# Attention in a three-part block: the probabilities turned by ordinary products with the identity instead of transposes

## The chip, the cores and the metric

The kernel runs on one core of a Trainium2 chip. The metric is the device time in microseconds of one execution. The engines are named as in the profile: PE is the matrix engine (PEld its loading of weights, which overlaps the products), DVE the vector engine, ACT the scalar engine, POOL the GpSimd engine, and SP starts the transfers that bring the weights into SBUF.

## What is computed

Three blocks follow each other on 256 tokens of width 1024: a block with three kinds of attention (compressed, selected, window), a block with dilated attention, and a third one with convolution, a gated delta rule and two feed-forward parts. All is float32. The change concerns only how two of the attention stages handle their probabilities. Cut to that, each head computes:

```python
# selected and window attention of the first block: 2 branches x 16 heads;
# dilated attention of the second block: 16 heads
s = jnp.einsum('bcghd,bkgd->bcghk', qq, kk) * scale
p = masked_softmax(s, mask)              # exp(s - max) / sum
o = jnp.einsum('bcghk,bkgd->bcghd', p, vv)
```

With 256 tokens, causality leaves three blocks of 128 queries by 128 keys for each head: the first 128 queries see the first 128 keys, the other 128 queries see all 256.

## The kernel before

The program is written out engine by engine. Each engine has its own list of instructions, and semaphores tie the lists together. A stage is over for PE when its last product is issued. PE goes from one stage to the next in this order: the projections of the first block with their turned operands, the compressed attention, the attention stage `nsa_att`, the output projection, then the same for the second block with `dil_att`, then the third block.

Both attention stages are objects of one class, `Attention`. Its `items` are the heads: 32 items in `nsa_att` (two groups of heads, two branches in each, eight heads) and 16 in `dil_att`. PE's list for them is a software pipeline over i:

- scores of item i (L828, L829): two products, with 64 rows of the array filled, since a head has 64 dimensions. The first makes 128 x 128 scores, the second 128 x 256. They go into bank i % 2 and wait until DVE has read item i - 2 (`masked_done`).
- the turned probabilities of item j = i - 2 (L837, 838): three blocks of 128 x 128 into bank 2 + j % 2, after ACT's exponentials of that item (`exp_done`) and after the turned blocks of item j - 2 have been copied out (`probsT_ready`). The probabilities are the weights that are loaded, the identity is the moving operand. The text below calls this group T(j).
- the products with v of item i - 3 (L849, L850, L851): three products with 64 moving columns each, whose weights are the turned probabilities. They add up in banks 4 to 7.

In the last iterations of a stage there are no scores left, so T and the products with v follow each other.

Beside it, DVE adds the mask to the scores and takes the maximum (L864, L866), makes the bias (L869), does one step of the modulation sums per item (`ada_beside`, L567), and copies out the turned blocks of every second item; after each eight items it weighs the sums (L1074, L1306). ACT does the exponentials (L891, L893) and copies out the turned blocks of the other items. These copies carry the line L527 of a helper. The next steps after the last item are a weighting on DVE, in the first stage an addition on POOL, and then the turning of the result and the output projection.

In all places other than this class, the kernel turns blocks in the helper `turn` with L514. The third block's delta rule contains ordinary products of 128 x 128 by 128 (L1940, L1945, L1994, L2002, L2010) and with 16 rows (L1930).

Of the kernel before, what the change touches and what calls it, by code (L numbers as in the profile page):

```python
# [12 lines left out]
P = 128  # L13
# [270 lines left out]
def build(nc, A, const_ap, out, last_block=2):  # L284
    ctx = ExitStack()
    with ctx:
# [9 lines left out]
        def C(name):  # L296
            a, b = CONST_AT[name]
            return const[:, a:b]

        ident, ones = C("ident"), C("ones")  # L300
# [28 lines left out]
        bank = [ctx.enter_context(nc.psum_tensor(f"bank{i}", [P, 512], F32))[:, :] for i in range(8)]  # L329
# [123 lines left out]
        lefts_used = set()  # L453

        def gemm(pe, stage, j, left, ready, n, kc_total=KC):


# [50 lines left out]
        def turn(pe, name, b, blocks):  # L508

            i = TURN_AT[name, b]  # L510
            if i >= 2:
                await_turns_read(pe, TURNS[i - 2][0], [TURNS[i - 2][1]])
            for src, kin, mout, col in blocks:
                mm = pe.transpose(bank[4 + i % 2][0:mout, col:col + kin], src, ident[0:kin, 0:kin])  # L514
            mm.then_inc(turned, 1)
# [280 lines left out]
        class Attention:  # L796
# [24 lines left out]
            def pe(self, pe):  # L821
                n = len(self.items)
                for i in range(n + 3):
                    if i < n:
                        q, k, _, _ = self.items[i]
                        if i >= 2:
                            pe.wait_ge(self.masked_done, i - 1)
                        pe.matmul(bank[i % 2][:, 0:P], q(0), k()[:, 0:P], start=True, stop=True)  # L828
                        pe.matmul(bank[i % 2][:, P:3 * P], q(1), k(), start=True,  # L829
                                  stop=True).then_inc(self.scored, 1)  # L830
                    if 2 <= i < n + 2:
                        j = i - 2
                        pe.wait_ge(self.exp_done, j + 1)
                        if j >= 2:
                            pe.wait_ge(self.probsT_ready[j % 2], j // 2)
                        for b in range(3):
                            mm = pe.transpose(bank[2 + j % 2][:, b * P:(b + 1) * P],  # L837
                                              self.probs[:, j % 2, b * P:(b + 1) * P], ident)
                        mm.then_inc(self.probs_turned, 1)
                    if i >= 3:  # L840
                        j = i - 3
                        g, c = j // 8, (j % 8) * DH
                        pe.wait_ge(self.probsT_ready[j % 2], j // 2 + 1)
                        if j % 8 == 0 and g >= 2:
                            pe.wait_ge(self.pv_read, g - 1)
                        v = self.items[j][3]
                        pT = self.probsT[:, j % 2, :]
                        o0, o1 = bank[4 + 2 * (g % 2)], bank[5 + 2 * (g % 2)]
                        pe.matmul(o0[:, c:c + DH], pT[:, 0:P], v(0), start=True, stop=True)  # L849
                        pe.matmul(o1[:, c:c + DH], pT[:, P:2 * P], v(0), start=True, stop=False)  # L850
                        pe.matmul(o1[:, c:c + DH], pT[:, 2 * P:3 * P], v(1), start=False,  # L851
                                  stop=True).then_inc(self.pv_done, 1)
# [1561 lines left out]
```

## Time and profile before

| | |
|---|---|
| median of 3 runs | 1487.2 us (1487.14 to 1492.58) |
| the profiled execution | 1491.99 us, span 1490.2 us |
| mean granted clock of PE | 0.862 of full speed |
| busy share of the span | PE 86%, PEld 71%, DVE 60%, ACT 35%, POOL 18% |
| instructions | PE 7557 products and 7557 weight loads, DVE 1465, ACT 875, POOL 154 |
| bytes from HBM | 219.27 MB, 148 GB/s over the span |

The profile shows one execution. Times are microseconds from the start of the span. A row of the timeline gives start, length, engine, line, operation, tiles, shape and the number of records it merges (x3); the length of a merged row runs from the first start to the last end. For a product the shape reads rows x columns of the weights, then the moving operand. "granted clock" is the share of PE's full clock that the chip allowed; its two levels are 0.5 (1.2 GHz) and 1.0 (2.4 GHz).

### The profile page before, as it was taken

How to read it: one execution, taken by the hardware profiler on the slowest of the kernel's cores; microseconds unless marked ns; L12 is line 12 of the kernel's file. 1: busy time of each engine (PE TensorE's matmuls, PEld its weight loads, DVE VectorE, ACT ScalarE, POOL GpSimd, SP SyncE). 2: the span in 40 equal slices, each digit the busy share in tenths (PEclk: the TensorE clock that was granted, in tenths of full speed). 3: DMA queues.
4: the chain of work that ended last, by engine and by line, in shares of the span. 5: the costliest groups of instructions: out<-in, count | busy, mean ns of one | idle time of the engine just before them, and what ended most of it. 6: DMA issues, size and time to landing. Idle time of an engine off the chain costs nothing. (4 is left out here: it accounts for less than half of the span.)

```text
span 1490.2 us, 19544 instructions
## 1 busy us (share of the span) xinstructions
PE 1275.6 (86%) x7557; PEld 1051.1 (71%) x7557; DVE 900.9 (60%) x1465; ACT 520.7 (35%) x875; POOL 264.5 (18%) x154
## 2 busy tenths in 40 slices
PE   1789699977888986999997988899989879799997
PEld 1565567765766764788785767678888877688885
DVE  5783556535985556595555578468655555555553
ACT  1231333323224333334433433533323233444441
POOL 0010001003542003334202432211030302100000
PEclk9989755578999557999998998879989989899998
DMA  8667342213776213487563444439600014455551
GB/s 290 237 226 243 102 126 73 71 43 112 229 242 208 98 57 110 154 291 230 182 201 104 135 123 127 142 123 300 240 2 2 3 58 142 127 177 183 197 164 71
DMA packets 142391, 221.59 MB, mean 149 GB/s; under 512 B 9735, under 2 KB 65627, under 8 KB 142171
## 3 DMA queue, kind: packets, MB, share of 16 engines
q1 hardware_dynamic: 139424, 216.37, 45.1%
q10 hardware_dynamic: 2875, 3.98, 0.8%
q8 instruction: 60, 0.98, 0.3%
q14 instruction: 32, 0.26, 0.1%
HBM read 219.27 MB, written 1.05 MB: 148 GB/s over the span
## 5 line engine op out<-in xcount | busy, mean ns | idle before, releaser
L479 PE MATMUL bank<-w_parts,lhs_hi 128*128 128x512 f32 (+2 forms) x960 | 397.5, 414 | 24.3 <-ACT w_parts L433 24.3
L433 ACT CAST w_parts<-ring 128x1024 fp32r<-128x1024 f32 (+2 forms) x288 | 288.9, 1033 | 344.9 <-PE bank L480 138.7
L438 DVE TENSOR_TENSOR w_parts<-ring,w_parts 128x1024 fp32r<-128x1024 f32 (+2 forms) x230 | 309.8, 1373 | 162.5 <-ACT w_parts L433 162.0
L480 PE MATMUL bank<-w_parts,lhs_lo 128*128 128x512 f32 (+2 forms) x960 | 390.6, 407 | 0.0
L487 PE MATMUL bank<-w_parts,lhs_hi 128*128 128x512 f32 (+2 forms) x960 | 262.8, 396 | 3.2 <-DVE w_parts L438 3.2
L479 PEld LDWEIGHTS bank<-w_parts,lhs_hi 128*128 128x128 f32 x960 | 191.2, 199 | 67.3 <-ACT w_parts L433 25.9
L480 PEld LDWEIGHTS bank<-w_parts,lhs_lo 128*128 128x128 f32 x960 | 191.8, 200 | 40.2
L487 PEld LDWEIGHTS bank<-w_parts,lhs_hi 128*128 128x128 f32 x960 | 184.9, 193 | 45.5 <-DVE w_parts L438 4.1
L438 POOL TENSOR_TENSOR w_parts<-ring,w_parts 128x1024 fp32r<-128x1024 f32 (+1 forms) x58 | 147.9, 2551 | 248.9 <-ACT w_parts L433 248.9
L567 DVE SCALAR_TENSOR_TENSOR ada_acc<-ring,c_act,ada_acc 128x512 f32<-128x512 f32 x210 | 172.9, 823 | 12.2 <-DMA ring<-in_w_ada 1.1
L762 POOL TENSOR_TENSOR x<-x,xn 128x512 f32<-128x512 f32 x20 | 30.1, 1524 | 415.3 <-DVE xn L754 415.3
L514 PE MATMUL bank<-const,arena 128*128 128x128 f32 (+2 forms) x322 | 58.0, 330 | 33.0 <-DVE arena L1336 6.8
L514 PEld LDWEIGHTS bank<-const,arena 128*128 128x128 f32 (+2 forms) x322 | 46.6, 172 | 42.8 <-DVE arena L1336 7.0
L590 PE MATMUL bank<-const,ada_acc 128*128 128x1 f32 x160 | 26.0, 284 | 50.5 <-DVE ada_acc L567 39.9
L479 PE MATMUL bank<-w_parts,up_hi 128*128 128x512 f32 x176 | 69.2, 393 | 0.0
L480 PE MATMUL bank<-w_parts,up_lo 128*128 128x512 f32 x176 | 68.7, 391 | 0.0
L1412 DVE TENSOR_TENSOR arena<-arena,bank 128x256 f32<-128x256 f32 x44 | 18.1, 420 | 83.0 <-ACT arena L1428 82.3
L590 PEld LDWEIGHTS bank<-const,ada_acc 128*128 128x128 f32 x160 | 25.8, 240 | 55.0 <-DVE ada_acc L567 35.3
L891 ACT ACTIVATE arena<-arena 128x128 f32<-128x128 f32 x48 | 19.3, 402 | 110.7 <-DVE arena L869 110.6
L514 PE MATMUL bank<-const,xn 128*128 128x128 f32 x80 | 19.8, 429 | 42.5 <-DVE xn L676 36.6
L864 DVE CUSTOM_DVE_ANT_0 arena<-bank,const 128x128 f32<-128x128 f32 x48 | 14.0, 291 | 66.3 <-PE bank L829 66.1
L1428 ACT ACTIVATE arena<-bank 128x256 f32<-128x256 f32 x44 | 16.8, 384 | 91.2 <-PE bank L487 89.6
(321 smaller groups left out, 1692.6 us busy)
## 6 DMA issues: line engine op xcount, KB each, us to landing
ring<-in_w_ffn_up SPq DMA_DIRECT2D x176, 256.0 KB, 3.8
ring<-in_w_ada SPq DMA_DIRECT2D x72, 512.0 KB, 4.7
ring<-in_ada_w SPq DMA_DIRECT2D x48, 512.0 KB, 4.8
ring<-in_w_ffn_down SPq DMA_DIRECT2D x44, 512.0 KB, 4.3
ring<-in_w_in SPq DMA_DIRECT2D x44, 512.0 KB, 4.0
ring<-in_dil_w_in SPq DMA_DIRECT2D x32, 512.0 KB, 4.1
ring<-in_nsa_w_in SPq DMA_DIRECT2D x20, 512.0 KB, 4.6
ring<-in_w_in SPq DMA_DIRECT2D x20, 416.0 KB, 4.2
```

Source lines behind the costliest of these rows:

```text
L433: eng.copy(hi, raw).then_inc(hi_ready, 1)
L438: eng.tensor_tensor(lo, raw, hi.bitcast(F32), ALU.subtract).then_inc(lo_ready[who], 1)
L479: pe.matmul(b, x_hi, w, start=(k0 + k == 0), stop=False)
L480: mm = pe.matmul(b, x_lo, w, start=False, stop=False)
L487: mm = pe.matmul(bank[2 * (o % 2) + tt][:, 0:n], x_hi, lo[:, k * n:(k + 1) * n], start=False, stop=(k0 + k == kc_total - 1))
L514: mm = pe.transpose(bank[4 + i % 2][0:mout, col:col + kin], src, ident[0:kin, 0:kin])
L567: ins = dve.scalar_tensor_tensor(acc, w, s, acc, ALU.mult, ALU.add)
L590: mm = pe.matmul(bank[7][:, c:c + 1], acc[:, c * P:(c + 1) * P], ones[:, 0:1], start=True, stop=True)
L762: pool.tensor_tensor(xs, xs, y_gated[:, tt, :], ALU.add).then_inc(x_ready, 1)
L891: act.activation(p[:, 0:P], m[:, 0:P], ACT.Exp, bias=self.bias[:, i, 0:1], scale=SCALE, accum_out=self.den[:, i, 0:1])
L1412: dve.tensor_tensor(up_h[:, j % 2, tt, :], up_a[:, j % 2, tt, :], gemm_bank(name + "_up", j, tt)[:, 256:512], ALU.mult).then_inc(bank_free ...
L1428: act.activation(up_a[:, j % 2, tt, :], gemm_bank(name + "_up", j, tt)[:, 0:256], ACT.Silu).then_inc(silu_done, 1)
```

## The change

In the turning step of the class `Attention`, `pe.transpose` is replaced by an ordinary `pe.matmul` with the same operands in the same roles: the block of probabilities as weights, the identity as moving operand, result into the same part of the same bank, each product starting and stopping its own sum. Waits, semaphores, order and all other engines stay as they are. The other places that turn blocks (`turn`, L514) keep the transpose.

```diff
@@ -834,8 +834,8 @@
                         if j >= 2:
                             pe.wait_ge(self.probsT_ready[j % 2], j // 2)
                         for b in range(3):
-                            mm = pe.transpose(bank[2 + j % 2][:, b * P:(b + 1) * P],
-                                              self.probs[:, j % 2, b * P:(b + 1) * P], ident)
+                            mm = pe.matmul(bank[2 + j % 2][:, b * P:(b + 1) * P],
+                                           self.probs[:, j % 2, b * P:(b + 1) * P], ident, start=True, stop=True)
                         mm.then_inc(self.probs_turned, 1)
```

## Rows read from the trace of the kernel before

**Rows 1.** The page's slices: granted clock, tenths of full speed, 40 slices of 37.3 us

```profile
PEclk9989755578999557999998998879989989899998
```

**Rows 2.** Windows: stretch, length, busy of PE PEld DVE ACT POOL, clock, DMA, GB/s

```profile
206.68:296.18 89.50, 89.50 (x327) 70.30 (x326) 51.44 (x175) 29.01 (x113) 7.48 (x6) 0.50 0.26 77
489.52:532.48 42.96, 42.96 (x158) 33.73 (x157) 22.57 (x85) 15.03 (x59) 0.00 (x0) 0.50 0.27 87
```

**Rows 3.** Timeline of PE, one item of the first stage and the next one's start

```profile
206.68 0.79 PE L828 MATMUL bank<-arena 64*128 64x128 f32 x2
207.27 1.06 PE L829 MATMUL bank<-arena 64*128 64x256 f32 x2
208.25 0.90 PE L837 MATMUL bank<-const,arena 128*128 128x128 f32 x3
208.95 0.53 PE L849 MATMUL bank<-arena,xn 128*128 128x64 f32 x2
209.27 0.64 PE L850 MATMUL bank<-arena,xn 128*128 128x64 f32 x2
209.69 0.63 PE L851 MATMUL bank<-arena,xn 128*128 128x64 f32 x2
210.26 0.79 PE L828 MATMUL bank<-arena 64*128 64x128 f32 x2
```

**Rows 4.** Waits between 206.68 and 296.18: us in total, times, longest

```profile
DVE arena L864 <- PE bank L829: 36.6, 22, 2.3
PEld bank L837 <- issue: 16.3, 25, 0.7
```

**Rows 5.** Line L837: count, duration ns min/median/max, first and last start

```profile
L837 PE MATMUL bank<-const,arena x144: 272/421/473, 195.1 to 538.2; 128*128 128x128 f32 x144
```

**Rows 6.** Timeline of PE at the start of the first and of the second stage

```profile
195.12 0.55 PE L837 MATMUL bank<-const,arena 128*128 128x128 f32 x3 [0.30 <-ACT arena L893]
195.60 0.54 PE L828 MATMUL bank<-arena 64*128 64x128 f32 x2
...
196.93 0.90 PE L837 MATMUL bank<-const,arena 128*128 128x128 f32 x3
198.05 0.69 PE L849 MATMUL bank<-arena,xn 128*128 128x64 f32 x2 [0.22 <-ACT xn L527]
...
488.69 0.90 PE L837 MATMUL bank<-const,arena 128*128 128x128 f32 x3
489.52 0.79 PE L828 MATMUL bank<-arena 64*128 64x128 f32 x2
```

**Rows 7.** Timeline of PE in the last items of the first stage

```profile
299.62 0.85 PE L837 MATMUL bank<-const,arena 128*128 128x128 f32 x3
300.26 0.53 PE L849 MATMUL bank<-arena,xn 128*128 128x64 f32 x2
```

**Rows 8.** Timeline of PE in the third block, ordinary products of 128 by 128 by 128

```profile
1131.93 2.07 PE L1994 MATMUL bank<-xn,lane_mem 128*128 128x128 f32 x8
1133.79 1.43 PE L1994 MATMUL bank<-xn,arena 128*128 128x128 f32 x8
...
1148.28 1.71 PE L1940 MATMUL bank<-arena 128*128 128x128 f32 x7
1149.78 1.92 PE L1945 MATMUL bank<-arena 128*128 128x128 f32 x8
```

**Rows 9.** Windows, columns as in rows 2, around three changes of the clock

```profile
158.00:165.20 7.20, 4.50 (x21) 4.06 (x22) 5.92 (x9) 1.98 (x3) 0.00 (x0) 0.50 0.68 215
165.30:168.00 2.70, 2.33 (x16) 1.52 (x15) 1.38 (x2) 1.17 (x2) 0.00 (x0) 1.00 1.02 382
1144.40:1147.90 3.50, 3.50 (x17) 2.81 (x16) 2.01 (x8) 1.28 (x8) 2.04 (x2) 1.00 0.00 0
1148.30:1151.30 3.00, 3.00 (x16) 3.00 (x16) 3.00 (x11) 1.59 (x6) 0.00 (x0) 0.50 0.00 0
1131.90:1133.79 1.89, 1.89 (x10) 1.87 (x9) 0.00 (x0) 0.76 (x2) 0.00 (x0) 0.50 0.00 0
1135.06:1138.00 2.94, 2.94 (x27) 2.78 (x25) 2.07 (x3) 0.00 (x0) 0.00 (x0) 1.00 0.00 0
```

**Rows 10.** Timeline of PE in two of these windows

```profile
162.40 3.40 PE L514 MATMUL bank<-const,arena 128*128 128x128 f32 x16
...
1144.40 3.71 PE L1930 MATMUL bank<-arena,const 16*128 16x256 f32 x16
```

## What the change should do to the time

> **What bounds the kernel now.** I read the page's slices first. The granted clock stands in their PEclk row, and it shows two long stretches at 0.5, slices 5 to 7 and slices 13 and 14 [rows 1]; these are the two attention stages, 32 items in the first and 16 in the second. Next I read the engines' busy time in the middle of each. In 89.50 us of the first, PE is busy for 89.50 us, DVE for 51.44 and ACT for 29.01, and the granted clock is 0.50 throughout, which is the 1.2 GHz level; the second stage is alike [rows 2]. So PE sets the pace, without a gap. The list of waits agrees: DVE waits for PE's scores, and the only thing before the turned blocks that is no work of PE is "issue", 16.3 us over 25 items [rows 4], which is time in which nothing that the profile shows was awaited.
>
> The timeline of one item gives the price list. An item runs from one start of L828 to the next, 206.68 to 210.26, which is 3.58 us; over the long stretch it is 89.50 / 25 = 3.58, over the second 42.96 / 12 = 3.58 [rows 2, 3]. Inside it the two score products start 0.59 and 0.98 us apart from what follows, the three transposes take 208.95 - 208.25 = 0.70 us, and the three products with v take 210.26 - 208.95 = 1.31 us [rows 3]. I use distances between starts and not durations, since durations overlap and their ends are modelled. The row's counts matter as well: one score product leaves two matmul records (x2), three transposes leave three (x3) [rows 3]. The 48 items thus have 144 transposes [rows 5].
>
> **What the change does to PE.** Both operands stay where they are, the probabilities as weights and the identity as moving operand; only the kind of instruction changes, on one line. Nothing is added on another engine, in a queue or in a wait. An ordinary float32 product leaves two records here, so 144 records become 288, each with its own weight load.
>
> The price of an ordinary product of just this shape, 128 rows, 128 columns, 128 moving columns, stands elsewhere in the trace at the same clock. L1994's first 8 records start at 1131.93 and the next form starts at 1133.79: 1.86 us [rows 8], at a granted clock of 0.50 [rows 9]. L1940 and L1945: 7 records from 1148.28 to 1149.78, so 1.50 / 7 = 0.214 us a record [rows 8]. If the other 7 of L1994 cost 0.213 each, the first costs 1.86 - 7 x 0.213 = 0.37: a record after a pause of the engine costs 0.16 more. So a turned block costs 2 x 0.213 = 0.427 us where it does not follow a pause.
> Today's transposes: in the last two items, where no score product stands ahead, three take 300.26 - 299.62 = 0.64 us, 0.213 each [rows 7]. With scores ahead they take 0.70, that is 0.05 more for the first [rows 3].
>
> Sum for an item with scores: the six records are 0.37 + 5 x 0.213 = 1.44 against 0.70, so +0.75 us, and the item goes from 3.58 to 4.33. For an item without: 6 x 0.213 - 0.64 = +0.64. Bounds: if ordinary products can start without the pause behind L829 (0.98 between L829 and L837 for 2 x 0.427 of streaming, so 0.13 of pause [rows 3]), the term is 0.75 - 0.13 - 0.16 + 0.05 = about 0.5 us; if the switch to the products with v costs another such pause, it is 0.75 + 0.13 = 0.88. I take 0.75, since L1994's row is the very shape and the pause also stands where score products follow products with v: L851's two records take 210.26 - 209.69 = 0.57 where 0.43 is the normal [rows 3]. It goes with the change from 64 rows to 128, which stays.
>
> What is hidden: DVE and ACT have 2.06 us (51.44 / 25) and 1.16 us of work in an item of 3.58 [rows 2], so neither ends a wait. At the first stage's start PE has gaps. T(0) at 195.12 runs at full clock, its three more records cost some 0.33, and the product that follows starts 0.48 later [rows 6], so most of that, 0.3, is passed on; T(1) starts at 196.93, ends 0.7 later and L849 starts at 198.05 [rows 6], so a gap of 0.4 swallows part of its 0.75. Together the two add about 0.65. At the second stage's start the transposes end against the next scores, 488.69 to 489.52 [rows 6], which is 0.70 and the pause; both count in full.
> First stage: 0.65 + 28 x 0.75 + 2 x 0.64 = 22.9. Second stage: 14 x 0.75 + 2 x 0.64 = 11.8. Sum **+34.7 us**. After each stage PE waits for a chain that starts at its last product with v, so the delay goes through to the end undiminished, and no engine works meanwhile on anything that could use the added time.
>
> The profiled execution took 1491.99 us (span 1490.2), the median is 1487.2, the three runs lie 5.4 us apart. Added to the profiled one the sum gives 1526.7; I give the forecast on the median: 1487.2 + 34.7 = **1521.9 us**.
>
> The Trainium skill speaks against this change: "Perfetto Trace Analysis", Optimizing Tensor Performance, Transposes, asks that a logical transpose be done as one and not as a standard matmul. "TensorE: Matmul & The Clock Gate", Terms, puts the transpose mode at 4 times faster for float32.
>
> **Rivals.** *The clock rises (faster).* In attention PE is busy without a gap and yet runs at 0.50. If the added products make the engine's work dense enough, the gate opens, and once open the whole item shrinks. Full-clock records lie 2.94 / 27 = 0.109 us apart in L2002 and L2010 [rows 9], so 4.33 becomes 4.33 x 0.109 / 0.213 = 2.22; DVE's 2.06 lies just below, say 2.25. With 10 of 48 items at the old clock the sum is 10 x 0.75 - 38 x 1.33 = -43 us: 1444 us. It decides from the point where at least 17 items run at full clock, since 31 x 0.75 = 23 = 17 x 1.33. For it: L1994 ran back to back at 0.50 and the clock was 1.00 by 1135.06 [rows 9]; turned blocks fill all 128 rows, and they go from 0.70 of 3.58 us to 1.44 of 4.33. Against it: transposes alone already raise the clock, L514's 16 from 162.40 on at 0.50, then 1.00 from 165.30 [rows 9, 10], so the time of T counts today and the swap adds no new kind of activity, it only doubles that part. And how many rows are filled matters: L1930, with 16 rows, kept PE busy for all of 1144.4 to 1147.9 at 1.00, and from 1148.3 the clock was 0.50 [rows 9, 10]. The scores fill only 64 rows for 1.57 us of each item, and the products with v pause half the time: 64 moving columns stream in half of their 0.213 us. Both remain. I give this 0.12.
> The same skill page, PE-mode transpose, says that the full clock does not engage for transposes. By that rule the swap would bring counted work where there was none, and this rival would be the likely one. Rows 9 and 10 show the clock rising behind transposes alone.
>
> *Four times.* An identity product could cost four passes of what a transpose costs: 3 x (4 x 0.213 - 0.213) = +1.92 us an item, 48 x 1.92 = +92: 1579 us. L1994's two records for a product at 0.213 each speak against it; 0.02. It is what the skill's factor would give.
>
> *Nothing changes.* If the float32 transpose had the same two passes hidden in its record, or the product came out as one record, the time would stay at 1487. The x2 of every ordinary product and the spacing of L1940 speak against it: 0.03.
>
> **How the numbers follow.** Forecast (+0.5 to +0.9 us an item) 0.81, clock rises 0.12, four times 0.02, nothing 0.03, something unseen 0.02. The bounds of the item's term give 42 x 0.5 + 4 = +25 and 42 x 0.88 + 5 = +42, and the runs of one kernel spread by 5 us; the upper bound is the less likely. The range 1511 to 1532 holds nearly all of the forecast's 0.81 and none of the others, so 0.8 in all. Faster by over 0.5% (7 us, about what a measurement of this kernel can tell from no change): 0.12; within it 0.03; slower 0.85.
>
> **What would show it.** In the profile after: L837 with 288 matmul records, 0.213 us apart, and as many weight loads; PEclk still 0.5 in both stages; an item of 4.33 us from L828 to L828; PE without a gap; DVE's wait for L829 longer by 0.75 an item; the stretch from the first L828 to the last L851 longer by 22.9 and 11.8 us; everything behind merely later. Wrong if PEclk shows 1.0 inside attention, if six records take other than 1.44 us, or if the stages gain different amounts than their item counts say.

## The result and the profile after

The changed kernel takes 1523.47 us (median of 4 runs, 1519.37 to 1525.46), the kernel before 1489.52 beside it. The ratio is 1.0222, with a 95% interval of 1.02 to 1.0245: slower by 33 us, between 30 and 36. The profiled execution took 1525.06 us, its span is 1523.2 against 1490.2.

The first view is the page's PEclk row of the changed kernel, to be laid beside [rows 1]:

```profile
PEclk9999655558989657799999899888989889899999
```

Both stages still stand at 0.5; since the slices are a little longer, the first stage is now slices 5 to 8 (the first slice is number 0). Then the windows in the middle of each stage (columns as in [rows 2]), the waits in the first of them, and the turning step's row (to be laid beside [rows 2, 4, 5]):

```profile
205.53:318.02 112.49, 112.49 (x417) 92.50 (x416) 53.00 (x181) 30.33 (x118) 7.47 (x6) 0.50 0.20 61
517.97:565.56 47.59, 47.59 (x177) 39.14 (x176) 20.17 (x74) 12.69 (x50) 0.00 (x0) 0.50 0.21 67
...
DVE arena L864 <- PE bank L829: 57.4, 26, 3.1
PEld bank L837 <- issue: 16.9, 26, 0.7
...
L837 PE MATMUL bank<-const,arena x288: 421/421/580, 195.3 to 573.5; 128*128 128x128 f32 x144
```

PE has no gap, and 112.49 / 26 = 4.327 us is an item. The wait of DVE for the scores is 57.4 / 26 = 2.21 us an item where it was 36.6 / 25 = 1.46: DVE got the 0.75 us as idle time. The 144 records of L837 have become 288. One item, as in [rows 3]:

```profile
205.53 0.79 PE L828 MATMUL bank<-arena 64*128 64x128 f32 x2
206.12 1.06 PE L829 MATMUL bank<-arena 64*128 64x256 f32 x2
207.11 1.65 PE L837 MATMUL bank<-const,arena 128*128 128x128 f32 x6
208.54 0.53 PE L849 MATMUL bank<-arena,xn 128*128 128x64 f32 x2
208.87 0.63 PE L850 MATMUL bank<-arena,xn 128*128 128x64 f32 x2
209.29 0.64 PE L851 MATMUL bank<-arena,xn 128*128 128x64 f32 x2
209.86 0.79 PE L828 MATMUL bank<-arena 64*128 64x128 f32 x2
```

The turning takes 208.54 - 207.11 = 1.43 us instead of 0.70; every other distance is the old one within a hundredth, the pause behind L829 included (0.99 from L829 to L837). The two places where a stage does not run in this rhythm are its ends. Here are the start of the first stage and the end of the second:

```profile
195.29 1.65 PE L837 MATMUL bank<-const,arena 128*128 128x128 f32 x6 [0.30 <-ACT arena L893]
196.88 0.79 PE L828 MATMUL bank<-arena 64*128 64x128 f32 x2
...
198.45 1.65 PE L837 MATMUL bank<-const,arena 128*128 128x128 f32 x6
199.89 0.53 PE L849 MATMUL bank<-arena,xn 128*128 128x64 f32 x2
...
573.70 0.40 PE L849 MATMUL bank<-arena,xn 128*128 128x64 f32 x2
573.93 0.39 PE L850 MATMUL bank<-arena,xn 128*128 128x64 f32 x2
574.16 0.39 PE L851 MATMUL bank<-arena,xn 128*128 128x64 f32 x2
574.55 0.43 PE L849 MATMUL bank<-arena,xn 128*128 128x64 f32 x2
```

T(0) now runs at the half clock: 1.59 us to the next scores where [rows 6] had 0.48. And the last products with v run at the full clock, 0.23 us a pair of records instead of 0.43.

To see where the 33 us came from I took, in each kernel, the start of the first L828 record and of the last L851 record of a stage from the timeline. The table has every kernel of this study; "rest" is the profiled span less the two stages. The ratios come from all runs but one, e5's slowest of four, 1481.46 us, which counts as a slow one.

| kernel | item, us | stage 1 | stage 2 | rest | ratio to before, interval |
|---|---|---|---|---|---|
| before | 3.58 | 113.1 | 55.9 | 1321.2 | |
| changed | 4.33 | 137.1 | 67.0 | 1319.1 | 1.0222 (1.02 to 1.0245) |
| e1, second stage alone | 3.58 / 4.33 | 113.1 | 67.8 | 1313.1 | 1.005 (1.003 to 1.0069) |
| e2, first block alone | 3.90 | 123.8 | 59.4 | 1317.1 | 1.0095 (1.0075 to 1.0115) |
| e3, last block alone | 3.79 to 3.80 | 120.4 | 58.5 | 1317.3 | 1.0039 (1.0022 to 1.0056) |
| e4, transposes twice | 4.22 | 133.2 | 65.1 | 1319.7 | 1.0181 (1.0161 to 1.0201) |
| e5, before with filler | 2.03, then 3.58 | 99.9 | 39.9 | 1317.9 | 0.989 (0.9826 to 0.9954) |
| e6, changed with filler | 2.33, then 4.33 | 117.6 | 38.8 | 1317.0 | 0.9894 (0.9858 to 0.9929) |
| e7, before, more filler | 2.03 | 75.9 | 35.7 | 1327.2 | 0.9647 (0.9611 to 0.9683) |
| e8, changed, more filler | 2.33 | 82.7 | 39.3 | 1319.7 | 0.9713 (0.9682 to 0.9745) |
| e9, e7 with a small addition | 2.03 | 73.6 | 35.7 | 1320.5 | one run |

For the changed kernel: stage 1 +23.9, stage 2 +11.2, rest -2.1, together the span's 33.0. The medians lie 34.0 us apart.

### The profile page after: what moved, and what is told of

Its sections match the earlier page's. It is cut to its first block and busy times, and to the rows that moved or that the text cites. A ratio compares the mean times of both kernels' runs of the same rounds, so it can differ in the third digit from the quotient of the medians.

```text
span 1523.2 us, 19832 instructions
## 1 busy us (share of the span) xinstructions
PE 1307.1 (86%) x7701; PEld 1083.1 (71%) x7701; DVE 904.0 (59%) x1465; ACT 520.6 (34%) x875; POOL 263.9 (17%) x154
## 3 DMA queue, kind: packets, MB, share of 16 engines
HBM read 219.27 MB, written 1.05 MB: 145 GB/s over the span
## 5 line engine op out<-in xcount | busy, mean ns | idle before, releaser
L438 DVE TENSOR_TENSOR w_parts<-ring,w_parts 128x1024 fp32r<-128x1024 f32 (+2 forms) x230 | 314.2, 1393 | 162.3 <-ACT w_parts L433 157.3
L514 PE MATMUL bank<-const,arena 128*128 128x128 f32 (+2 forms) x322 | 58.4, 333 | 34.6 <-DVE arena L1336 6.8
L837 PEld LDWEIGHTS bank<-const,arena 128*128 128x128 f32 x288 | 65.1, 326 | 28.7 <-issue 26.0
L837 PE MATMUL bank<-const,arena 128*128 128x128 f32 x288 | 78.8, 447 | 0.3 <-ACT arena L893 0.3
L514 PEld LDWEIGHTS bank<-const,arena 128*128 128x128 f32 (+2 forms) x322 | 46.8, 172 | 44.2 <-DVE arena L1336 6.9
L590 PE MATMUL bank<-const,ada_acc 128*128 128x1 f32 x160 | 25.6, 281 | 50.4 <-DVE ada_acc L567 40.0
L590 PEld LDWEIGHTS bank<-const,ada_acc 128*128 128x128 f32 x160 | 25.2, 236 | 55.4 <-DVE ada_acc L567 35.9
```

What stands on the lines that cost most here:

```text
L438: eng.tensor_tensor(lo, raw, hi.bitcast(F32), ALU.subtract).then_inc(lo_ready[who], 1)
L590: mm = pe.matmul(bank[7][:, c:c + 1], acc[:, c * P:(c + 1) * P], ones[:, 0:1], start=True, stop=True)
L837: mm = pe.matmul(bank[2 + j % 2][:, b * P:(b + 1) * P], self.probs[:, j % 2, b * P:(b + 1) * P], ident, start=True, stop=True)
```

## Experiments

The theory to test: in both stages PE is alone the bound, at the half clock; each turned block has one more record, and each further record costs 0.213 us. The rivals: the price hangs on the change of kind between instructions; the ordinary product as such is dear; part of the 33 us is a shift of the clock elsewhere. And then the question that the prediction left with a chance of 0.12: what holds the clock at 0.5 in stages where PE never rests?

**One stage alone (e1).**

```diff
-                            mm = pe.transpose(bank[2 + j % 2][:, b * P:(b + 1) * P], ...
+                            if self.name == "dil_att":
+                                mm = pe.matmul(bank[2 + j % 2][:, b * P:(b + 1) * P], ...
+                            else:
+                                mm = pe.transpose(bank[2 + j % 2][:, b * P:(b + 1) * P], ...
```

> Only the 16 items of the second stage (dil_att) are turned by ordinary products; the 32 of the first keep the transposes. Theory (each further record of a turned block costs PE 0.213 us at the half clock, and nothing hides it): +11.2 us, all of it between the first L828 and the last L851 of the second stage; an item of 4.33 us there and of 3.58 us in the first. Rival (a good part of the added 33 us is a shift of the clock's steps elsewhere in the program, not the items): the second stage grows by about 11, but the whole by clearly more or less.

Measured: the stage grew by 67.8 - 55.9 = 11.9 us where I expected 11.2 (the prediction had said 11.8), its items are 4.33 us, the first stage is unchanged to a hundredth. The whole is slower by 0.5%, 4.5 to 10.3 us, and that interval leaves 11.2 out. The rest of the profiled span is 8.1 us shorter, although its instructions are the same. So the items cost what the theory says, and the rival is right in its smaller part: the rest of the program moves by some microseconds from kernel to kernel, more than I had allowed for.

**One block of three, first or last (e2, e3).** As in e1, with `b == 0` or `b == 2` as the condition.

> Only the first of the three blocks of each item is an ordinary product. Theory (records, and 0.10 us more where the first record stands behind PE's pause): item with scores 3.58 + 0.31 = 3.89 us, item without +0.21; 44 x 0.31 + 4 x 0.21 = +14.5 us. Rival (going from one kind of instruction to the other makes PE pause by 0.13 us, as it does behind L829): item 4.02, +20.8 us.

> Only the last of the three blocks of each item is an ordinary product. Theory: one more record of 0.213 us in each of 48 items, item 3.79 us, +10.2 us, so 0.10 us an item less than with the first block, though the work is the same. Rival (the place does not matter, every block has the same price): as with the first block, a third of 0.75, item 3.83 us, +12. Rival (change of kind costs a pause): item 3.93, +16.5 us.

An item of each (e2, then e3; L838 is the ordinary product, L841 the transpose):

```profile
209.35 0.79 PE L838 MATMUL bank<-const,arena 128*128 128x128 f32 x2
209.94 0.64 PE L841 MATMUL bank<-const,arena 128*128 128x128 f32 x2
210.37 0.53 PE L853 MATMUL bank<-arena,xn 128*128 128x64 f32 x2
```

```profile
208.37 0.69 PE L841 MATMUL bank<-const,arena 128*128 128x128 f32 x2
208.86 0.64 PE L838 MATMUL bank<-const,arena 128*128 128x128 f32 x2
209.28 0.53 PE L853 MATMUL bank<-arena,xn 128*128 128x64 f32 x2
```

In e2 the product takes 0.59 us behind the pause and the two transposes 0.43; in e3 the transposes take 0.49 behind the pause and the product 0.42. The items are 3.90 and 3.80 us against 3.89 and 3.79 expected, the stages together +14.2 and +10.0 against 14.5 and 10.2. No pause shows between the kinds in either direction, and the place does matter by 0.10 us: a first record behind the pause is dearer by that much when it belongs to a product. Of the whole, e2 has all of it (+14.1); e3 has 5.8 us (3.3 to 8.3), again less than its stages.

**Transposes twice (e4).**

```diff
-                        for b in range(3):
+                        for b in (0, 1, 2, 0, 1, 2):
```

> The three transposes of each item are done twice over, into the same places: six records as in the changed kernel, but all of them transposes. Theory (the number of records sets the price, the kind only touches the first one after a pause): item 3.58 + 0.64 = 4.22 us, 48 x 0.64 = +30.7 us, granted clock 0.5 in both stages as in the changed kernel. Rival (the ordinary product itself is dear): clearly less than +30, near +15. Rival (transposes do not count for the clock, products do): the clock's course in the stages differs from that of the changed kernel.

```profile
210.04 1.06 PE L829 MATMUL bank<-arena 64*128 64x256 f32 x2
211.03 1.54 PE L837 MATMUL bank<-const,arena 128*128 128x128 f32 x6
212.36 0.52 PE L849 MATMUL bank<-arena,xn 128*128 128x64 f32 x2
```

Six transpose records take 1.33 us, six product records 1.43; the item is 4.22 us, the stages together +29.3 (expected 30.7), the whole 24 to 30 us slower. So it is the number of records, and the kind only makes the first one dearer by 0.10. In the middle of the first stage the clock is 0.50 as in the changed kernel:

```profile
205.00:318.00 113.00, 113.00 (x430) 92.24 (x429) 53.94 (x187) 30.90 (x120) 7.48 (x6) 0.50 0.19 61
```

**Filler ahead of the stages (e5, e6).** At the start of a stage PE stands still while the first items pass through DVE and ACT. If the clock is lost there, work that nobody reads should keep it. e5 puts it into the kernel before, e6 into the changed one:

```diff
+                    for _ in range(self.filler.get(i, 0)):   # i = 1: 4 in stage 1, 2 in stage 2
+                        pe.matmul(bank[7][:, :], ident, self.filler_src(), start=True, stop=True)
 ...
             await_turns_read(pe, "dil_k", range(4))
+            for _ in range(10):
+                pe.matmul(bank[7][:, :], ident, dil_att.filler_src(), start=True, stop=True)
             pe.wait_ge(mod_ready, 18)
```

> The kernel before (transposes), with products that nobody reads where PE would stand still ahead of the items: four products of 128 by 128 by 512 in the first stage behind the scores of item 1, ten ahead of the second stage's wait and two behind the scores of its item 1. Theory (the clock falls at the start of each stage because PE waits while the pipeline fills, and it follows what PE does, transposes included): with the idle time filled, the stages start at 1.0. If items with transposes then hold it, an item costs PE 3.58 x 0.109 / 0.213 = 1.83 us and DVE's 2.06 us sets the pace: about 2.1 us an item, 1487 - 46 x 1.45 = about 1420 us. If they do not hold it, the clock drops back within some us and the time is 1487 to 1491. I hold the second for the likelier: an item at 2.1 us has the same work in less of full rows than the changed kernel. Rival (attention runs at the half clock whatever stands ahead of it): item 3.58 throughout, 1489 us.

> The same filler in the changed kernel (ordinary products). Theory (twice the records with all rows filled keep the clock up once it is up): the stages hold 1.0, an item costs PE 4.33 x 0.109 / 0.213 = 2.2 us against DVE's 2.06, so about 2.25 us; against the kernel before 46 x 1.33 = -61 us: about 1426 us, faster than both kernels. Rival (half clock whatever stands ahead): item 4.33, about 1524 us. If both this and the transposes with filler hold the clock, the kind of the turning does not matter for the clock and the transposes win by the smaller item.

Both are faster than the kernel before by about 1% (e5 by 0.5 to 1.7, e6 by 0.7 to 1.4), with more work in them. Both are far from the 1420 and 1426 us of the theory: the median of the three runs in e5's ratio is 1464.65 us, that of e6's four 1473.67. In e5 the first stage ran at the full clock from its start to 218.2 us, with intervals of 1.95 and 2.11 us between items in turn, then at the half clock with 3.58; in e6 to 223.7 us with 2.33, then 4.33. My likelier case for e5, a fall within some microseconds, did not come, and for e6 I had expected the full clock through the whole first stage. The profile of e5 is that of its fastest run, 1459.52 us; where the others lost the clock no trace shows. The second stage of e6 held the full clock to its end, that of e5 to its last two items. What ended it in e5's first stage:

```profile
214.58 2.49 POOL L1169 TENSOR_TENSOR arena<-arena,xn 128x512 f32<-128x512 f32 x2 [92.72 <-DVE xn L1076]
215.02 0.85 DVE L871 TENSOR_SCALAR arena<-arena 128x2 f32<-128x2 f32 x1
215.78 1.83 DVE L567 SCALAR_TENSOR_TENSOR ada_acc<-ring,c_act,ada_acc 128x512 f32<-128x512 f32 x1
217.31 0.43 PE L851 MATMUL bank<-arena,xn 128*128 128x64 f32 x2 [2.04 <-ACT xn L527]
```

Behind the eighth item of a group DVE weighs the sums and POOL adds them up; DVE falls back, ACT with it, and PE stands still for 2.04 us ahead of a product with v; from 218.2 us on the clock is 0.50. In the second stage of e5 the same wait is 1.15 us, and the first of these two windows holds it:

```profile
494.70:498.10 3.40, 2.25 (x15) 1.61 (x15) 3.33 (x14) 2.33 (x9) 0.00 (x0) 0.99 0.36 131
498.10:505.00 6.90, 6.90 (x28) 5.48 (x28) 3.45 (x14) 2.33 (x9) 0.00 (x0) 0.50 0.23 76
```

PE is busy for 2.25 of 3.40 us at the full clock, then comes the half clock, at which it is busy without a gap and does not get back. In the second stage of e6 the longer turning fills most of this wait, 0.15 us of it are left, and the clock holds. (In e6's first stage 1.05 us of the wait were left, at 223.42 us, and the clock fell at 223.7.)

```profile
493.00:531.00 38.00, 37.81 (x254) 30.32 (x250) 28.17 (x108) 20.74 (x75) 0.00 (x0) 1.00 0.36 112
```

So the rival of the prediction has a true part: in this one pair of stages the kernel with the added records kept a clock that was up. More than that is not shown.

**More filler (e7, e8).** So the next step fills that wait too:

```diff
+                        if i % 8 == 5 and i >= 13:
+                            for _ in range(self.filler_late):   # 8 in stage 1, 4 in stage 2
+                                pe.matmul(bank[2 + j % 2][:, 3 * P:4 * P], ident, self.filler_src()[:, 0:P],
+                                          start=True, stop=True)
                         for b in range(3):
```

> Transposes, the filler of e5, and in iterations 13, 21 and 29 of a stage eight (second stage: four) more products of 128 by 128 by 128 that nobody reads, ahead of the turning. Those are the iterations in which PE waits for a copy because DVE is weighing a group of eight items; in the profile of e5 the clock fell in just such a wait, at item 13 of the first stage and near the last items of the second. Theory (the clock is lost in those waits): the clock stays at 1.0 through both stages, items of 2.0 us as in e5, the first stage about 113.1 - 38 = 75 us long, the second about 37: about 1430 us in all. Rival (the clock does not hold for more than some 30 us with items of this kind, whatever the waits): it falls at about item 13 again, 1468 us as in e5.

> The same filler with the ordinary products of the changed kernel. Theory: clock 1.0 through both stages; e6 showed items of 2.33 us at the full clock against 1.95 to 2.11 with transposes, so 32 x 0.30 + 16 x 0.30 = 14 us above the transposes with the same filler, about 1444 us: the change costs 0.3 us an item at the full clock where it costs 0.75 at the half. Rival (at the full clock DVE sets the pace of both and the products cost nothing): the same time as with transposes.

The PEclk rows of the pages, e7 and then e8, and a window over nearly all of e7's first stage:

```profile
PEclk9989789889899889999999998899898989899998
```

```profile
PEclk9999789898899988999998998899999999899999
```

```profile
194.00:269.00 75.00, 73.40 (x466) 55.28 (x464) 64.44 (x223) 37.38 (x144) 7.50 (x6) 1.00 0.40 124
```

The stretches at 0.5 are gone. The stages are 75.9 and 35.7 us long in e7 (expected 75 and 37), 82.7 and 39.3 in e8. e7 is faster than the kernel before by 3.5% (3.2 to 3.9), 49 us by the medians (1438.94 against 1487.92, expected about 1430), and is the best version of this study; e8 is faster by 2.9% (median 1443.89, expected about 1444). What the two runs do not separate is whether the clock held because PE no longer stood still or because of the kind of product that was put there. The items' price at the full clock, from e8 and from e7 (turning is L843, its product with v L855):

```profile
216.02 0.49 PE L828 MATMUL bank<-arena 64*128 64x128 f32 x2
216.35 0.59 PE L829 MATMUL bank<-arena 64*128 64x256 f32 x2
216.87 0.94 PE L843 MATMUL bank<-const,arena 128*128 128x128 f32 x6
217.64 0.33 PE L855 MATMUL bank<-arena,xn 128*128 128x64 f32 x2
...
218.35 0.49 PE L828 MATMUL bank<-arena 64*128 64x128 f32 x2
```

```profile
218.53 0.49 PE L828 MATMUL bank<-arena 64*128 64x128 f32 x2
...
219.38 0.55 PE L843 MATMUL bank<-const,arena 128*128 128x128 f32 x3
219.76 0.33 PE L855 MATMUL bank<-arena,xn 128*128 128x64 f32 x2
...
220.47 0.48 PE L828 MATMUL bank<-arena 64*128 64x128 f32 x2
```

Six product records take 0.77 us, and an item 218.35 - 216.02 = 2.33 us, in which PE sets the pace. With transposes the three records take 219.76 - 219.38 = 0.38 us where nothing is waited for, and items follow each other at 1.94 and 2.11 us in turn, 2.03 on average; in every second one PE waits a little for the copy of the turned blocks ahead of L855. So with products the turning costs PE 0.39 us more at the full clock, and on average 0.09 of it goes into that wait: 0.30 us an item, against 0.75 at the half clock. The stages differ by 6.8 + 3.6 = 10.4 us, less than my 14. One reason is in the long intervals, those with the filler: they are 4.12 us in e8 and 4.19 to 4.25 in e7's first stage, so there the products cost nothing.

**A small addition on POOL (e9).** POOL adds one head of eight instead of all in L1169 (here L1173). The kernel leaves out seven eighths of the addition, so it is a measuring device and no version to be used; it ran once.

> The kernel e7 with POOL's addition of each group's result (L1169 in e5) done for one head of eight, so seven eighths of it are left out. In e5 DVE's instructions beside that addition took 0.85 and 1.83 us where they take 0.17 and 0.74 otherwise. Theory (DVE is slowed while POOL adds, and this lengthens the wait in which PE stands still): these two go back to about 0.17 and 0.75, and the long interval between the scores of items 13 and 14, 4.25 us in e7, shrinks to the 3.36 us of the second stage, where POOL does nothing. Rival (the long interval is DVE's weighing alone): it stays near 4.2.

```profile
219.05 0.60 POOL L1173 TENSOR_TENSOR arena<-arena,xn 128x64 f32<-128x64 f32 x2 [97.05 <-DVE xn L1080]
219.19 2.05 PE L840 MATMUL bank<-arena,const 128*128 128x128 f32 x16
...
219.49 0.18 DVE L875 TENSOR_SCALAR arena<-arena 128x2 f32<-128x2 f32 x1
219.59 0.74 DVE L567 SCALAR_TENSOR_TENSOR ada_acc<-ring,c_act,ada_acc 128x512 f32<-128x512 f32 x1
```

Both DVE instructions are back at their usual length, so the long addition on POOL was what slowed them. (In e5's first stage the two are long beside each of POOL's three pairs of additions, 0.78 to 0.85 and 1.83 us.) The interval between the items shrank from 4.25 to 3.78 us and not to 3.36. I had forgotten the filler: its 16 records stand in this interval, 8 in the second stage's, and the next transposes start 1.89 us behind them, at 221.08. An item's own 1.94 us and these 1.89 make 3.83, and PE waits for nothing in the interval: it is PE's own work now.

## Why the prediction was right

The forecast was 34.7 us more, and 33 came. The mechanism was the forecast one; that the sum came out so near is in part luck, since the start of the first stage (+1.0 us against the forecast), the second stage (-0.6) and the rest (-2.1) partly cancel out.

*What bounds the stages*: right. PE without a gap at 0.50 in both kernels, and DVE's idle time took the added 0.75 us.

*The term of the sum*: right to 0.01. Forecast 1.44 us for six records and 4.33 an item, measured 1.43 and 4.327. The pause behind L829 stayed and none came towards the products with v, so the term stayed clear of both bounds, 0.5 and 0.88 us. e2 and e3 show both parts apart, 0.213 for a record and 0.10 for a first one.

*The start of the first stage*: mis-sized. I priced T(0) at the full clock, +0.3 us; it cost 1.59 - 0.48 = 1.11. In [rows 6] T(0) still ran at the full clock; in the profile after, the clock had fallen by then. The same happened in e2, e3 and e4 but not in e1, whose first stage is that of before; what decides it is not shown. T(1) cost 1.44 - 1.12 = 0.32 as forecast. So the stage grew by 23.9 instead of 22.9.

*The second stage*: 11.8 forecast, 11.2 measured. The difference is at the end, where the clock rose for the last products with v: the last two groups of products with v start 0.85 us apart, 573.70 and 574.55, where it was 1.18 in the kernel before. e1, in which the clock did not rise there, shows 11.9. The tail is the one place in the stage without scores.

*The rest*: "merely later" was too simple. 2.1 us less in this profile, 8.1 less in e1, and in the eleven profiles from 1313.1 to 1327.2 us, for the same instructions but for ten products in e5 to e9 and the shorter additions in e9. That spread is larger than the effect of e3. It was luck that the changed kernel's rest came out near that of before.

*The rival "the clock rises"*: in the changed kernel it did not, but for the second stage's last products. My arguments were that the scores fill only half of the rows and that the products with v pause. No run changes the filled rows or the moving columns, so neither argument is tested: [rows 9, 10] show a fall behind products with 16 rows, but not that the rows were the reason. Why a stage in which PE never rests stays at 0.50 remains open. What the runs show is another condition that I had not seen: both forms of the items kept the full clock once they had it and the waits were filled (e7, e8), and as long as there were scores neither got it back from the half clock. It was lost behind PE's waits at a stage's start and at a group of eight. The sentence that a whole item would shrink to 2.22 us was close (2.33), and its price of 43 us for that case comes near the 44 us between e8 and before. That second agreement is a coincidence in part: the rival left 10 items at the half clock, and e8 has none of them but pays for its filler.

*Transposes and the clock.* "Transposes alone" was too strong for [rows 9, 10]: eight small products of L590, with one moving column, run from 160.70 us on, ahead of them. The trace of e5 has a cleaner place, the same turning, in which PE runs only transposes for 4.5 us before the clock rises:

```profile
158.48 6.07 PE L514 MATMUL bank<-const,arena 128*128 128x128 f32 x28
...
159.00:163.50 4.50, 4.50 (x21) 3.56 (x20) 1.87 (x3) 1.42 (x3) 0.00 (x0) 0.50 0.95 317
163.70:165.10 1.40, 1.21 (x10) 0.80 (x9) 0.69 (x1) 0.66 (x2) 0.00 (x0) 1.00 1.05 399
```

The Trainium skill, "TensorE: Matmul & The Clock Gate", PE-mode transpose, says that the full clock does not engage for transposes. These rows don't agree. Nor does anything in the attention stages bear it out: e7 keeps 1.00 through a window of 75 us with transposes in every item, and e4, with twice the transposes, stands at 0.50 in the middle of the first stage as the changed kernel does. The same page of the Trainium skill, Terms, gives the transpose mode a factor of 4 for float32. Measured it is 2 here, two records of 0.213 us against one. The Trainium skill's rule to turn with transposes and not with standard matmuls ("Perfetto Trace Analysis", Optimizing Tensor Performance, Transposes) holds in its direction: the products cost 33 us here.

## What to carry to other kernels

Price a change of a matrix-engine instruction by the distance between starts in a row of the same shape at the same granted clock, and count records: here an ordinary float32 product is two, a transpose one. Before pricing anything in a stage where the engine is busy throughout, look at whether it is busy at the half clock. If it is, look for the short waits behind which the clock was lost: they can be worth more than the instructions in the stage. Filling them with products that nobody reads brought 49 us here, more than the change had cost.

## What the hardware showed that I had not expected

- A stage can run at the half clock for over 100 us with PE busy throughout, and at the full clock with the same items when its first waits and three later ones are filled with products that nobody reads: 113.1 and 75.9 us for the same 32 items.
- DVE slows down beside POOL: a small operation took 0.85 us instead of 0.17 and a 128x512 one 1.83 instead of 0.74 while POOL added 128x512 values; with 128x64 on POOL both were normal (one run).
- Identical code outside the stages took between 1313.1 and 1327.2 us from profile to profile. The clock's course explains this only in part: outside the stages it stood at the half level for 246 us in the kernel before and for 231 us in e1, whose rest is 8.1 us shorter, but for 235 us in the changed kernel, whose rest is only 2.1 us shorter.
- The full clock can come behind transposes alone: in e5, 4.5 us of them at 0.50, then 1.00.
